# Feed-forward gate and up projections of pairs 2 to 10 as seven half-size block products

## What is computed

```
def _conv_ffn(h, w_in, conv_w, conv_b, w_out):
    gate, up = _split_cols(h @ w_in, (D_FF, D_FF))
    gate = _causal_dwconv(gate, conv_w, conv_b)          # 3 taps along the tokens
    return (jax.nn.gelu(gate) * up) @ w_out

        gt, up = jnp.split(h @ w_ffn_in[l], 2, axis=-1)
        x = x + (jax.nn.silu(gt) * up) @ w_ffn_out[l]
```

## Time and profile before

| | us |
|---|---|
| median of 3 runs | 3122.77 |
| lowest and highest | 3120.22, 3125.18 |
| span of the profiled execution (first to last instruction) | 3119.4 |
| PE busy in that span | 3097.3 |
| DVE, ACT, POOL busy | 1563.7, 1063.2, 237.6 |

### The profile page before, as it was taken

The page is one execution under the profiler, slowest core; times in us unless marked ns, Lnnn a source line. Parts: engine busy times, 40 slices in busy tenths (PEclk is TensorE's granted clock), DMA queues, the critical chain, the costliest instruction groups (busy, mean ns, idle before and its releaser), DMA issues.

```text
span 3119.4 us, 37101 instructions
## 1 busy us (share of the span) xinstructions
PE 3097.3 (99%) x15540; PEld 2594.3 (83%) x15540; DVE 1563.7 (50%) x1889; ACT 1063.2 (34%) x1155; POOL 237.6 (8%) x139
## 2 busy tenths in 40 slices
PE   9999999999999999999999999999999999999999
PEld 7798988888889798888888778888888878888887
DVE  7564555554335554555435764544433766444432
ACT  3223343443223433444323332333323332333321
POOL 0002100010000020010000000111000000100100
PEclk9999999999999999999999999999999999999999
DMA  4412412223321131222233122222232322222222
GB/s 170 115 55 73 144 55 90 99 94 108 120 97 68 48 142 55 85 99 99 95 108 116 58 92 101 90 99 93 103 108 89 95 82 95 95 95 96 94 106 95
DMA packets 47567, 297.72 MB, mean 95 GB/s; under 512 B 7075, under 2 KB 7331, under 8 KB 13396
## 3 DMA queue, kind: packets, MB, share of 16 engines
q1 hardware_dynamic: 42336, 285.91, 25.9%
q10 hardware_dynamic: 5108, 10.02, 1.4%
HBM read 291.16 MB, written 4.75 MB: 95 GB/s over the span
## 4 chain that ended last, share of the span: by engine, by line
PE 91%; DVE 5%; ACT 2%; issue 1%; DMA 0%; ACTq 0%; POOL 0%; DVEq 0%; SPq 0%
PE G L460 83%; DVE wL L1688 1%; ACT wH L1255 1%; PE psS L816 1%; DVE mxt L1920 1%; PE psS L520 1%; PE psS L1017 1%; PE psS L1134 0%; PE G L1143 0%; PE G L1024 0%; PE psT L552 0%; DVE ws L2477 0%; PE psT L1170 0%; PE G L1058 0%; PE psS L949 0%
## 5 line engine op out<-in xcount | busy, mean ns | idle before, releaser
L460 PE MATMUL G<-hH,wH 128*128 128x512 f32 x2560 | 1015.4, 397 | 9.1 <-DVE wL L1688 3.9
L460 PE MATMUL G<-hH,wL 128*128 128x512 f32 x2560 | 998.8, 390 | 0.0
L460 PE MATMUL G<-hL,wH 128*128 128x512 f32 x2560 | 997.7, 390 | 0.0
L1688 DVE TENSOR_TENSOR wL<-raw,wH 128x2048 fp32r<-128x2048 f32 x260 | 626.5, 2410 | 634.3 <-ACT wH L1255 634.0
L460 PE MATMUL G<-wsr,wH 128*128 128x512 f32 (+1 forms) x2512 | 745.9, 380 | 0.4
L1255 ACT ACTIVATE wH<-raw 128x2048 fp32r<-128x2048 f32 x263 | 501.7, 1908 | 591.7 <-PE G L460 573.1
L460 PEld LDWEIGHTS G<-hH,wH 128*128 128x128 f32 x2560 | 481.5, 188 | 124.1 <-issue 20.3
L460 PEld LDWEIGHTS G<-hH,wL 128*128 128x128 f32 x2560 | 481.0, 188 | 102.3
L460 PEld LDWEIGHTS G<-hL,wH 128*128 128x128 f32 x2560 | 481.9, 188 | 97.9 <-issue 1.2
L460 PEld LDWEIGHTS G<-wsr,wH 128*128 128x128 f32 x2512 | 464.3, 189 | 91.0 <-issue 1.5
L460 PE MATMUL G<-wsr,wL 128*128 128x512 f32 (+1 forms) x1256 | 476.1, 379 | 0.0
(11 more groups left out here) (291 smaller groups left out, 2510.3 us busy)
## 6 DMA issues: line engine op xcount, KB each, us to landing
raw<-in_units SPq DMA_DIRECT2D x263, 1024.0 KB, 4.8
ws<-bias_rows SPq DMA_DIRECT2D x2, 1536.0 KB, 14.7
bias_rows<-ws ACTq DMA_DIRECT2D x1, 2560.0 KB
x<-in_x SPq DMA_DIRECT2D x4, 512.0 KB, 7.5
ws<-in_mem ACTq DMA_DIRECT2D x2, 1024.0 KB, 4.7
ws<-bias_rows ACTq DMA_DIRECT2D x1, 2048.0 KB, 8.2
out_x<-x SPq DMA_DIRECT2D x3, 512.0 KB, 7.1
ws<-in_decay ACTq DMA_DIRECT2D x1, 1280.0 KB, 7.6
```

What stands on the lines that cost most here:

```text
L460: mm = pe.matmul(o, mv if swap else wt, wt if swap else mv, start=first and n == 0, stop=last and n == 2)
L1688: V.tensor_tensor(wL[:, g.p, :], raw[:, g.p, :], wH[:, g.p, :].bitcast(F32), ALU.subtract)\
```

## The change

Pairs 0 and 1 of each feed-forward layer stay as they are. In pairs 2 to 10 gate and up are computed together as one 2 x 2 block product. The input is cut in blocks by k (k-tiles 0 to 3 and 4 to 7) and by tokens (0 to 255 and 256 to 511), the weights by k and by up and gate. Winograd's form of Strassen's scheme makes seven products of blocks in place of eight; each is 4 k-tiles x 2 output tiles x 3 matmuls of 256 columns, 24 matmuls. The seven forms of the input (three blocks, one of them negated, and four sums) are made once a layer: DVE normalises the input fully (L2241, eight ops), POOL makes the sums `S1` to `S4` (L3081), ACT and DVE their high and low parts (L1534, L2209, L2211). For each pair POOL makes four sums of weight blocks (L3089 to L3102), ACT and DVE split seven half units (L1547, L2218) into a ring of three, ACT copies three partial results out of PSUM (L1555) and one quarter of the result (L1562), DVE adds the other three quarters (L2229). Both units of a pair are loaded together, into `raw` for even and into the memory of `hH` and `hL` (`rawx0`, `rawx1`) for odd pairs. PSUM banks alternate between `psS`, `psT` and `G`. The high and low parts of all hidden tiles are made at the end, ACT's from the last pair on, POOL's (L3105) after its last sums. The loops over pairs are written out. The first product of a pair needs the raw up block of k-tiles 0 to 3, the second that of 4 to 7. In the diff below the parts stand in this order: the table of products, PE, the table of weight blocks, DVE at the entry, POOL for each pair.

```
+PRODUCTS = (("A11", "X", True), ("A12", "Y", True), ("S2", "X", False), ("S1", "V", True), ("S3", "X", False),
+            ("S4", "V", False), ("A22", "X", False))
...
             def ffn(f, final=False):
                 first_jobs()
-                with c.repeat(FT // 2 - 1, job=2, unit=2):
-                    plain(h_op)
+                for n in range(2 * FIRST_PAIRS - 2):
                     plain(h_op)
...
+                for m in range(FAST):
...
+                        pe.wait_ge(tl_ready, g + 1)
+                        tH, tL = ring[g % 3]
+                        for k in range(4):
+                            for t in range(2):
+                                w0 = k * 256 + t * P
+                                o = banks[m % 2][at][:, t * 256:t * 256 + 256]
+                                for p_, (w, h) in enumerate(((tH, formH), (tH, formL), (tL, formH))):
+                                    mm = pe.matmul(o, w[:, w0:w0 + P], h[form][:, k, :],
...
+        def blocks_of(m):
+
+            up_, gate_ = pair_raw[m % 2]
+            return (up_[:, lower], up_[:, upper], t_two(m), t1buf, t3buf[:], gate_[:, upper], t_two(m))
...
+                step(scaled(tn[:]), unit=False)
+                split()
+                for k in range(KT):
+                    ins = V.scalar_tensor_tensor(normed_h[:, k, :], x[:, k, :], own(k), rbt, ALU.mult, ALU.mult)
...
+                if l is not None:
+                    taps(0, 1, 1)
+                    taps(0, 0, 2)
+                step(scaled(hidden[0]), unit=False)
+                product(0)
+                split()
+                form("A11")
+                form("A12")
+                form("S1")
+                dve.wait_ge(act_g, FT // 2 * f + 1)
+                step(scaled(tn[:]), unit=False)
+                low_block(7 * first)
+                form("S2")
+                form("S3")
...
+                for m in range(FAST):
...
+                    W.tensor_tensor(t1buf, gate_[:, lower], up_[:, lower], ALU.subtract).then_inc(t_made, 1)
...
+                    W.tensor_tensor(t_two_m, gate_[:, upper], t1buf, ALU.subtract).then_inc(t_made, 1)
...
+                    W.tensor_tensor(t3buf[:], gate_[:, upper], gate_[:, lower], ALU.subtract).then_inc(t_made, 1)
+                    pool.wait_ge(tl_ready, 7 * n + 3)
+                    W.tensor_tensor(t_two_m, t_two_m, up_[:, upper], ALU.subtract).then_inc(t_made, 1)
+                for j in range(FT // 2):
+                    pool.wait_ge(ah_ready, FT // 2 * f + j + 1)
+                    W.tensor_tensor(hidL[j], hidden[j], hidH[j].bitcast(F32), ALU.subtract).then_inc(al_ready, 1)
```

More of the change, by code:

```diff
@@ L406, in _, with load_unit @@
                 sp.dma_start(dst, s_).then_inc(par_in, 16)
[L407 to L413 removed]
+            def load_unit(n, of, dst):
+                sp.dma_start(dst, a["units"][of]).then_inc(raw_in[n % 2], 16)
@@ L421, in _ @@
                                 .then_inc(c_in[part], 16)
[L422 to L427, removed]
+                    sp.wait_ge(wl_ready, n - 1)
+                    load_unit(n, of, raw[:, n % 2, :])
+                    n += 1
+                jobs += JOBS_2
+                ffn_loads(2 + l, n, order[ins_at], jobs - 8)
+                n += 2 * FIRST_PAIRS + 12
             for m in range(3):
@@ L1247, in _, with split @@
             activation = nc.scalar.activation
-            def split(done=job_done, count=None):
+            def split(done=job_done, count=None, src=None):
                 g = c.unit
@@ L1377, in pair_step, with form @@
[L1377 to L1385, removed]
+                def form(name):
+                    if name[0] == "S":
+                        act.wait_ge(sum_made, 4 * f + int(name[1]))
+                    else:
+                        act.wait_ge(n_ready, 2 * f + (1 if name == "A11" else 2))
+                    activation(formH[name], form_src[name], ACT.Copy, scale=-1.0 if name == "A22" else 1.0)\
+                        .then_inc(form_h, 1)
@@ new lines, in hidden_high @@
+                def hidden_high(j):
+                    act.wait_ge(hid_ready, FT // 2 * f + j + 1)
+                    act.wait_ge(prod_done, 7 * (first + FAST - 1) + HIDDEN_AFTER[j])
+                    activation(hidH[j], hidden[j], ACT.Copy).then_inc(ah_ready, 1)
+                act.wait_ge(job_free, jobs + 3)
+                gated(0)
+                split(job_done, jobs + 1)
+                gelu(0)
+                form("A11")
+                split(job_done, jobs + 2)
+                for name in ("A12", "S1", "S2", "S3"):
+                    form(name)
@@ L1386, in ffn @@
+                n = first + FAST - 1
+                act.wait_ge(c_read, 3 * n + 3)
+                gated(FT // 2 - 1)
+                last_quarter(n)
+                split(prod_done, 7 * n + 7, pair_raw[1][1])
+                for j in range(7, FT // 2 - 1):
+                    hidden_high(j)
+                gelu(FT // 2 - 1)
+                hidden_high(FT // 2 - 1)
                 residual(pieces=True, gain=gain, final=final)
@@ L1957, in ffn @@
+                if l is not None:
+                    taps(FT // 2 - 1, 1, 1)
+                    taps(FT // 2 - 1, 0, 2)
+                split(pair_raw[1][1])
+                product(FT // 2 - 1)
                 if before:
@@ L2764, in _ @@
             c.sq.off, c.bc.off, c.row.off, c.piece.off = 0, 0, 0, 0
-            for l in c.layers(2, chain=CHAIN_P, job=JOBS_2, stat=6, hd=FT // 2, lay=1, mg=8, mh=4):
+            for l in c.layers(2, chain=CHAIN_P, job=JOBS_2, stat=6, lay=1, mg=8, mh=4):
                 rstd(rsb, ST)
@@ L2786, in _ @@
                 rstd(rsb, ST)
-                ffn()
-                c.job.off += 4 + 22 + 4
+                ffn(2 + l, sum(JOBS_1) + (l + 1) * JOBS_2 - 8)
+                c.job.off += 4 + 4 + 4
 def _columns(v):
```

421 lines of the change are left out of this document (352 added, 69 removed).

## The result

The changed kernel takes **3204.6 us** (median of 4 runs, 3200.15 to 3205.53) against 3121.8 (3120.22 to 3125.18), a ratio of 1.0262 with an interval of 1.0247 to 1.0276. The forecast was 3203, range 3100 to 3232. The profiled execution has a span of 3202.6 us, 83.2 more than before.

What follows compares the result with a forecast made beforehand. TensorE (PE), busy 99%, bounds the kernel; 57.6 us could be saved there, but DVE-POOL exclusion makes it wait: +39.6 us per first-block layer, +0.4 per second-block layer, twice each +80 on 3122.8, giving 3203 us, range 3100 to 3232.

Steps and rivals of the forecast that it cites:

- fourth job and handover: Layer entry: PE waits for DVE's split of the fourth unit; 10.4 us per layer in the first block, 2.3 in the second.
- first Strassen pair: Each layer's first pair in the new scheme, with PE waiting on DVE and POOL: 33.8 us first block, 29.9 second.
- PE's sum: TensorE's matmul time per pair of units: 21.76 us becomes 20.16, saving 57.6 us over 36 pairs if PE never waits.
- rival of slower matmuls: Strassen products: 256-column matmuls run slower in this order; break-even 129.5 ns against 120.0, counted in the upper tail.
- DVE and POOL exclude each other: Two-SBUF-tile DVE ops and POOL ops never run together; first asker goes first, 0.15 us of a waiting start hidden.
- gain rival: POOL's sums don't hold DVE up, so pairs take 20.16 us in both blocks: 3075 us, chance 0.13.
- entry's layout: First-block entry: DVE's normalising ops, four taps alternating with three POOL sums, then splits; fourth unit 10.2 us late.
- rival of taps apart: Taps and normalising ops don't take part in the DVE-POOL exclusion, pairs 20.16 us in both blocks: 3136 us, chance 0.11.
- DVE keeps its turn: DVE holds its turn while ops are queued, putting POOL off into DVE's waits: 3135 or 3147 us, chance 0.08.
- Steady pair: Later Strassen pairs: 22.9 us in the first block, set by DVE and POOL; 20.16 in the second, PE not held up.
- The rest of the kernel stays: Everything outside the feed-forward layers was predicted to keep its time; extra instruction fetch from written-out loops costed at nothing.
- Second: ... +0.4: Each second-block feed-forward layer was put at 196.2 us against 195.8 before, a loss of 0.4.

Runs made afterwards that it cites:

- experiment 1: Against the changed kernel, POOL's four weight-block sums per pair made 2 columns wide instead of 1024 from each layer's third Strassen pair on: 3169.8 us.
- experiment 2: Against the changed kernel, POOL's four weight-block sums per pair replaced by copies of one SBUF tile each: 3126.6 us.
- experiment 5: Against the changed kernel, all input and weight-block sums moved from POOL to DVE, POOL keeping only the hidden tiles' lows: 3149.0 us.
- experiment 3: Against the changed kernel, unused matmuls keep PE busy in its two longest waits of each first-block layer: 3206.4 us.
- experiment 4: Against the changed kernel, Strassen's scheme only in the second block's two layers, the first block as before the change: 3127.4 us.

## Why the prediction was right, and where its terms were off

Per layer, us; measured from starts of PE's matmuls in the trace of the change:

| term | predicted | measured |
|---|---|---|
| first block: fourth job and handover, beyond PE's own | 10.4 | 10.3, 11.2 |
| first Strassen pair | 33.8 | 32.0, 32.6 |
| second | 21.6 | 21.2, 21.2 |
| six steady pairs | 137.4 | 134.5, 134.5 |
| last pair | 28.4 | 29.3, 29.3 |
| down projection, beyond PE's own | 5.7 | 5.9, 5.9 |
| whole layer against before | +39.6 | +35.3, +36.8 |
| second block: fourth job and handover | 2.3 | 2.0, 3.0 |
| first Strassen pair | 29.9 | 29.7, 31.2 |
| seven steady pairs | 141.1 | 141.1, 141.1 |
| last pair | 22.9 | 23.2, 25.5 |
| whole layer against before | +0.4 | +0.2, +5.3 |
| outside the layers | 0 | +5.6 |

- **PE's sum** holds: a product is 2.88 us, a pair without waits 20.16, in every second-block layer. The rival of slower matmuls is out.
- **DVE and POOL exclude each other**: confirmed in both directions (experiments 1, 2 and 5), and it decides the sign. The gain rival would have needed low blocks of 1.23 us; their groups have means of 1.36 to 2.11.
- **The terms of waits agree better than the waits do.** In both first-block layers the fourth job starts 8.7 us late, not 10.2; the 10.3 and 11.2 come about because that job is then 1.6 and 2.5 us longer at the lower clock. In the entry's layout POOL gets in between the four taps three times (3.0 + 6.7 us); in the trace they take 7.0, with two of POOL's sums in between, and the fourth sum holds up the split behind them (3.80 us instead of 2.2). In the first Strassen pair the waits, counted from starts, are 9.2 and 9.1 us, not 13.6, and slow matmuls add 2.6 and 3.4. The down projection waits 4.1, not 5.7, and slow matmuls add 1.7.
- **Taps take part**: the rival of taps apart (3136) is refuted by the 3.55 us for two. That DVE keeps its turn is refuted by the same row: POOL got in between two taps that were both ready.
- **Steady pair**: 22.4 on average and not 22.9; lengths are 21.1, 22.3 and 23.8. The first Strassen pair was put 1.2 to 1.8 too long. With all terms the two first-block layers were 7 us too dear. (The densest slice of the earlier trace rows is 389 GB/s and not 384; it changes the second load by less than 0.1.)
- **"The rest of the kernel stays"** was off by 5.6 us in this trace, and "Second: ... +0.4" by 4.9 in the last layer. The first is no cost of the change. The kernels of experiment 3 and of the change have the same instructions ahead of the first feed-forward layer; in the trace of experiment 3 that layer starts 0.3 us later than in the kernel before, in the change's 4.1 later. Of 255 to 300 us the windows have (kernel before, the change, experiment 3):

```profile
255.00:300.00 45.00, 43.37 (x212) 36.26 (x212) 16.70 (x26) 13.25 (x17) 11.40 (x10) 0.92 0.12 42
```

```profile
255.00:300.00 45.00, 43.37 (x202) 36.71 (x202) 15.23 (x21) 11.61 (x13) 9.36 (x7) 0.85 0.07 24
```

```profile
255.00:300.00 45.00, 43.37 (x213) 36.21 (x214) 16.96 (x25) 13.14 (x17) 11.10 (x9) 0.92 0.12 39
```

Nothing that runs there was edited in any kernel; the granted clock is 0.85 to 0.92 in the ten traces, and the first layer's window starts between 489.5 and 493.8 us: a difference between executions, as the 5 us between the runs of the kernel before are. Of the second block, experiments 3 and 4 and the change have the same instructions: the third layer takes 360.8, 358.0 and 357.9 us in them, the fourth 362.9, 361.6 and 362.8. So the forecast of +0.4 held for the third layer within the 2.9 us that it varies by, and not for the fourth. In the change the fourth layer differs from the third by 3.7 us of slower matmuls and 1.4 of longer waits. What makes the fourth the longer one in all three was not tested, so the cause of its 5 us stays open.

So 80 against 83.2 is partly luck: the waits were put too long, and the lower clock, which the forecast leaves out, filled the place. The forecast had 80 + 57.6 = 137.6 us more of waits. Counted from the starts of matmuls, the trace has 99 us more of waits (95.7 by the page's idle time), 33 more of matmuls at the lower clock and 9 of small steps, together 141, less the 57.6 saved. The 33 are 244 matmuls of Strassen products that start 213 ns apart instead of 120, and 105 of 512 columns at 427 instead of 227, of which the kernel before has 55. Where DVE sets the time the slower matmuls only fill PE's waits (experiment 3, up to the sixth product); behind the last wait of a stretch they cost their full length. How much of the 33 us reached the end was not separated.

## What to carry to other kernels

Work that is given to GpSimd to relieve VectorE can cost VectorE more than doing it itself: here each sum on GpSimd holds VectorE off for up to 2.24 us (1.6 on average, the estimate of experiment 5) against 1.23 on VectorE. Add the hold times of both engines before splitting elementwise work between them, and put on GpSimd what meets no operation of VectorE on two SBUF tiles. A scheme that saves matmuls is worth what its first and last steps leave of it: in the second block its seven steady pairs gained 11 us per layer and entry and last pair lost them, until the sums were on VectorE and the order of the two feeding engines was laid out for it.

## What was not expected of the hardware

- **The granted clock falls after PE has waited.** After the 8.55 us wait the fourth job starts like this:

```profile
533.83 0.79 PE L572 MATMUL G<-hH,wH 128*128 128x512 f32 x1 [8.55 <-DVE wL L1943]
534.42 0.63 PE L572 MATMUL G<-hL,wH 128*128 128x512 f32 x1
534.85 0.63 PE L572 MATMUL G<-hH,wL 128*128 128x512 f32 x1
535.27 0.63 PE L572 MATMUL G<-hH,wH 128*128 128x512 f32 x1
```

Starts lie 427 ns apart instead of 227; the mean granted clock of the whole job is 0.87, a mixture of 1.2 and 2.4 GHz. With PE kept busy in the same wait it was 1.00 (experiment 3). The Trainium skill, "TensorE: Matmul & The Clock Gate", section "Wait — 56ns, not 53.3ns?", has N / 1.2 ns between starts at the lower clock, which agrees with 213 and 427. At the full clock its N / 2.4 + 2.5 would be 109 and 216 ns; these fp32r matmuls show 120 and 227, and the measurement decides.
- **A copy on POOL is short**: 1.05 us for 1024 elements, where a sum of two tiles takes 2.41 alone. It holds DVE off all the same, for its shorter time.
- **How much a pair's length swings**: with identical work, the first block's steady pairs are 21.1, 22.3 or 23.8 us, and they follow from PE's wait and the clock. The 22.3 us pair has one wait of 1.9. The 23.8 has the same wait and 1.5 us of slower matmuls after it (granted clock 0.93 instead of 1.00). The pair after that one waits only 0.7 and takes 21.1.
